# Up and down products with one 512-column matmul per weight tile, folded by ACT and DVE

## The reference, cut to what matters

```python
def _conv_ffn(h, w_up, conv_w, conv_b, w_down):
    a, g = jnp.split(h @ w_up, 2, axis=-1)
    a = lax.conv_general_dilated(a, conv_w[:, None, :], window_strides=(1,),
                                 padding=[(CONV_W - 1, 0)], dimension_numbers=('NWC', 'WIO', 'NWC'),
                                 feature_group_count=D_FF) + conv_b
    return (jax.nn.gelu(a) * g) @ w_down
...
y = _conv_ffn(h, w_up[l], conv_w[l], conv_b[l], w_down[l])
x = x + g2 * _rmsnorm(y, norm_g[l, 3])
```

## Time and profile before

| | us |
|---|---|
| median of three runs | 758.73 |
| lowest and highest | 753.63, 760.63 |
| span of the profiled execution | 757.1 |
| that execution's own time | not listed |
| PE busy (x5964) | 730.8 (97%) |
| PE weight loads busy | 710.5 (94%) |
| DVE busy | 524.7 (69%) |
| ACT busy | 396.1 (52%) |
| POOL busy | 104.3 (14%) |

### The profile page before, as it was taken

How to read it: one execution, slowest core, us unless ns; L and a number is a source line. 1 busy time by engine, 2 the same in 40 slices (tenths; PEclk the granted TensorE clock), 3 DMA queues, 4 the chain that set the end, 5 groups by cost and what they waited for, 6 DMA issues and landing times.

```text
span 757.1 us, 14222 instructions
## 1 busy us (share of the span) xinstructions
PE 730.8 (97%) x5964; PEld 710.5 (94%) x5964; DVE 524.7 (69%) x778; ACT 396.1 (52%) x560; POOL 104.3 (14%) x87
## 2 busy tenths in 40 slices
PE   8899999998899999999999999999999999999995
PEld 6799899898898999999999989899999999999995
DVE  4979888886977678777767556925576347555665
ACT  4286455545364544544544348528555456556551
POOL 0130000000522000000001130000004455443000
PEclk9999999999999999999999999979999999999998
DMA  8995567555363455654566544514446553343101
GB/s 343 411 356 190 203 268 274 193 204 219 113 244 146 167 200 190 213 178 161 204 261 233 205 138 148 207 66 168 167 154 223 184 206 117 116 159 112 57 1 56
DMA packets 22265, 141.13 MB, mean 186 GB/s; under 512 B 2389, under 2 KB 3029, under 8 KB 6458
## 3 DMA queue, kind: packets, MB, share of 16 engines
q1 hardware_dynamic: 21626, 137.28, 50.1%
q0 software_dynamic: 576, 2.95, 1.0%
HBM read 139.17 MB, written 1.05 MB: 185 GB/s over the span
## 4 chain that ended last, share of the span: by engine, by line
PE 70%; DVE 13%; issue 7%; ACT 5%; DMA 3%; POOL 0%; SPq 0%; DVEq 0%; ACTq 0%
PE res L1596 20%; PE res L1598 19%; PE res L1597 19%; ACT whi L639 3%; DVE wlo L1052 3%; PE pX L1803 2%; DMA shared<-in_w_ada 1%; PE pS L1783 1%; PE pX L1982 1%; DVE shared L1065 1%; DVE raw L1065 1%; DMA y<-in_w_ada 1%; ACT sq L654 1%; PE pT L1793 1%; PE pS L1644 1%
## 5 line engine op out<-in xcount | busy, mean ns | idle before, releaser
L1596 PE MATMUL res<-hhi,whi 128*128 128x256 f32 (+1 forms) x1120 | 318.9, 285 | 4.1 <-DVE wlo L1052 1.5
L1052 DVE TENSOR_TENSOR wlo<-raw,whi 128x2048 fp32r<-128x2048 f32 (+3 forms) x101 | 229.1, 2270 | 126.4 <-ACT whi L639 126.2
L1597 PE MATMUL res<-hhi,wlo 128*128 128x256 f32 (+1 forms) x1120 | 312.9, 279 | 0.0
L1598 PE MATMUL res<-hlo,whi 128*128 128x256 f32 (+1 forms) x1120 | 312.8, 279 | 0.0
L639 ACT ACTIVATE whi<-raw 128x2048 fp32r<-128x2048 f32 (+3 forms) x101 | 188.3, 1865 | 120.2 <-issue 87.1
L1596 PEld LDWEIGHTS res<-hhi,whi 128*128 128x128 f32 (+1 forms) x1120 | 209.6, 187 | 5.9 <-issue 3.4
L1597 PEld LDWEIGHTS res<-hhi,wlo 128*128 128x128 f32 (+1 forms) x1120 | 209.4, 187 | 0.4
L1598 PEld LDWEIGHTS res<-hlo,whi 128*128 128x128 f32 (+1 forms) x1120 | 209.4, 187 | 0.2
L538 POOL TENSOR_TENSOR sq<-sq,rope 128x512 f32<-128x512 f32 x18 | 39.5, 2195 | 78.5 <-ACT sq L654 78.5
L1596 PE MATMUL res<-uhi,whi 128*128 128x256 f32 x176 | 49.3, 280 | 0.0
L1597 PE MATMUL res<-uhi,wlo 128*128 128x256 f32 x176 | 49.1, 279 | 0.0
(11 more groups left out here) (334 smaller groups left out, 1211.1 us busy)
## 6 DMA issues: line engine op xcount, KB each, us to landing
raw<-in_wts SPq DMA_DIRECT2D x97, 1024.0 KB, 5.0
raw<-in_w_ada SPq DMA_DIRECT2D x16, 1024.0 KB, 5.1
shared<-in_w_ada SPq DMA_DIRECT2D x6, 1024.0 KB, 11.1
gates<-in_wts SPq DMA_DIRECT2D x4, 768.0 KB, 13.3
raw<-in_wts SPq DMA_DIRECT2D x4, 768.0 KB, 5.6
y<-in_w_ada SPq DMA_DIRECT2D x2, 1024.0 KB, 9.2
x<-in_xT SPq DMA_DIRECT2D x2, 512.0 KB, 4.7
gv<-in_ln_rows POOLq DMA_DIRECT2D x1, 1024.0 KB, 7.5
```

The source lines that it names most:

```text
L1052: nc.vector.tensor_tensor(lo[:, 0:b], raw[RAW_OF["w", c] % RAW][:, 0:b], hi[:, 0:b].bitcast(f32), ALU.subtract).then_inc(lo_ready, 1)
L1596: mm(out, ah, bh, start=first, stop=False)
L1597: mm(out, al, bh, start=False, stop=False)
L1598: return mm(out, ah, bl, start=False, stop=last)
```

## The change

- The up and down products use `wide` in place of `three`: one matmul of the high weights with the 512 columns [high input | low input] into a whole bank (A | B), and one of the low weights with the high input (256 columns) into A. For this the high and low tiles of each operand lie in one tensor (`hs`, `us`, `wsplit`, and others that are only renamed). The rest of the kernel keeps `three`.
- Bank places: even up chunks and even down blocks in pS (one bank per 128 outputs), odd ones in pT. PE waits for the drain two chunks (or two blocks) back.
- ACT copies the B halves to `side` (`copy_side`), DVE adds A and `side` (`fold`, `fold_up`): into `aseq`, into a new `gsum`, or into `y`. All results of up and down are now drained by DVE.
- ACT makes the first tap of the convolution (scale and bias), DVE the other two, those of the two tiles in turn, so that a tap doesn't wait for the one just ahead of it.
- In the steps of up DVE makes the low half of chunk b + 2 in place of b + 3, behind the fold, and `ulo` of a pair a step later than before.
- In down ACT squares and scales `y` in SBUF after the fold.
- `turned` at up chunk 2 is gone.

```diff
-    if c < MISC or BRANCH <= c < WOUT or (UP <= c < DOWN and (c - UP) % 2 == 1):
+    if c < MISC or BRANCH <= c < WOUT or UP <= c < GK:
         return "dve"
...
+        def wide_banks(c):
+            n = (c - UP) % 2 if c < DOWN else (c - DOWN) // 3 % 2
+            return (pS, pT)[n]
+        def wide_part(c, i, e):
+            return wide_banks(c)[:, :].rearrange("p (i e n) -> p i e n", i=2, e=2)[:, i, e, :]
...
+            def copy_side(c, i):
+                nc.scalar.activation(side_of(c)[:, i, :], wide_part(c, i, 1), ACT.Copy).then_inc(side_copied, 1)
+                if UP <= b < DOWN:
+                    act.wait_ge(product_done, RESULT_MARK[FIRST_RESULT[b]])
+                    if b >= UP + 2:
+                        act.wait_ge(drained_dve, RESULT_DRAIN[FIRST_RESULT[b - 2]][1])
+                    copy_side(b, slice(0, 2))
                 if b not in LATE and b not in (GOUT + 1, GOUT + 2) and b != WOUT + 2 and b >= DIRECT:
                     high(c + 2)
...
-                        nc.scalar.activation(aseq[:, j % 2, :, 2:T + 2], ps[:, :].rearrange("p (a b) -> p a b", a=2),
-                                             ACT.Copy).then_inc(drained_act, 1)
+                        act.wait_ge(drained_dve, RESULT_DRAIN[FIRST_RESULT[b]][1])
+                        for i in range(2):
+                            f = 2 * j + i
+                            nc.scalar.activation(conv[:, j % 2, i, :], aseq[:, j % 2, i, 0:T], ACT.Identity,
+                                                 scale=col("conv_w", f), bias=col("conv_b", f)).then_inc(conv_first, 1)
...
+                        act.wait_ge(product_done, RESULT_MARK[FIRST_RESULT[b] + i])
+                        if j >= 2:
+                            act.wait_ge(drained_dve, RESULT_DRAIN[FIRST_RESULT[b - 6] + i][1])
+                        copy_side(b, slice(i, i + 1))
+                    for i in range(2):
+                        act.wait_ge(drained_dve, RESULT_DRAIN[FIRST_RESULT[b] + i][1])
+                        nc.scalar.activation(sq[:, 2 * j + i, :], y[:, 2 * j + i, :], ACT.Square).then_inc(squares["n4"], 1)
...
+                        nc.scalar.activation(y[:, 2 * j + i, :], y[:, 2 * j + i, :], ACT.Copy,
+                                             scale=pcol[:, 3, 2 * j + i:2 * j + i + 1]).then_inc(y_scaled, 1)
...
+            def fold(c, i, dst):
+                return nc.vector.tensor_tensor(dst, wide_part(c, i, 0), side_of(c)[:, i, :], ALU.add)
+            def fold_up(c, dst):
+                dve.wait_ge(side_copied, copies(c))
+                fold(c, slice(0, 2), dst).then_inc(drained_dve, 1)
+                if UP <= b < DOWN:
+                    j = (b - UP) // 2
+                    if (b - UP) % 2 == 0:
+                        fold_up(b, aseq[:, j % 2, :, 2:T + 2])
+                        if j:
+                            u_low(j - 1)
+                    else:
+                        fold_up(b, gsum[:, :, :])
+                    if b > UP:
+                        low(c + 1)
+                if b == DOWN:
+                    u_low(FT // 2 - 1)
+                    low(c + 1)
...
-                            own(nc.vector.tensor_scalar(o, a[:, 0:T], col("conv_w", f), col("conv_b", f), ALU.mult, ALU.add))
-                            own(nc.vector.scalar_tensor_tensor(o, a[:, 1:T + 1], col("conv_w", FT + f), o, ALU.mult, ALU.add))
+                        for a, o, f in taps:
+                            nc.vector.scalar_tensor_tensor(o, a[:, 1:T + 1], col("conv_w", FT + f), o, ALU.mult, ALU.add
+                                                           ).then_inc(dve_self, 1)
+                        for i, (a, o, f) in enumerate(taps):
+                            dve_count[0] += 1
+                            dve.wait_ge(dve_self, dve_count[0])
+                            ins = nc.vector.scalar_tensor_tensor(o, a[:, 2:T + 2], col("conv_w", 2 * FT + f), o, ALU.mult, ALU.add)
...
-                        nc.vector.tensor_tensor(g, g, ps[:, :], ALU.mult).then_inc(drained_dve, 1)
+                        g = gelu[:, j % 2, :, :]
+                        nc.vector.tensor_tensor(g, g, gsum[:, :, :], ALU.mult).then_inc(u_full, 1)
...
+            def wide(out, a, b, first, last):
+                mm(out.rearrange("p (e n) -> p e n", e=2), a[:, 0, :], b, start=first, stop=False)
+                return mm(out[:, 0:T], a[:, 1, :], b[:, 0, :], start=False, stop=last)
+            def wide_half(c, i, k, inp, at):
+                return wide(wide_banks(c)[:, 512 * i:512 * i + 512], weights_of(c)[:, :, k, i * P:i * P + P], inp[:, :, k, :],
+                            at == 0, at == KT - 1)
...
                     elif c > UP + 1:
-                        if c == UP + 2:
-                            turned(c)
-                        fm(c, hhi, hlo)
+                        wait_weights(c)
+                        wait_drained(FIRST_RESULT[c - 2])
+                        for i in range(2):
+                            for k in range(KT):
+                                last = wide_half(c, i, k, hs, k)
+                        last.then_inc(product_done, 1)
                 elif c < GK:
...
+                    if kg == 0:
+                        wait_drained(FIRST_RESULT[UP + 20 + j] if j < 2 else FIRST_RESULT[DOWN] + 2 * (j - 2) + 1)
                     for i in range(2):
-                        ps = bank(r + i) if kg == 0 else res[(r + i) % NB]
+                        ps = wide_banks(c)[:, 512 * i:512 * i + 512]
...
-                            last = three(ps[:, 0:T], wh[:, k, i * P:i * P + P], wl[:, k, i * P:i * P + P],
-                                         uhi[:, kk, :], ulo[:, kk, :], kk == 0, kk == FT - 1)
+                            last = wide(ps, wp[:, :, k, i * P:i * P + P], us[:, :, kk, :], kk == 0, kk == FT - 1)
```

More of the change, by code:

```diff
@@ L296, in build @@
         with ExitStack() as st:
-            uhi = sb("uhi", [P, FT, T], f32r, at=st)
-            ulo = sb("ulo", [P, FT, T], f32r, at=st)
+            us = sb("us", [P, 2, FT, T], f32r, at=st)
+            uhi, ulo = us[:, 0, :, :], us[:, 1, :, :]
             aseq = sb("aseq", [P, 2, 2, T + 2], at=st)
@@ L1057, in result, with u_low @@
                 return place(r)
+            def fold(c, i, dst):
[3 more added lines that the diff above has]
+                fold(c, slice(0, 2), dst).then_inc(drained_dve, 1)
+            def u_low(j):
+                dve.wait_ge(u_hi, j + 1)
+                nc.vector.tensor_tensor(ulo[:, 2 * j:2 * j + 2, :], gelu[:, j % 2, :, :],
+                                        uhi[:, 2 * j:2 * j + 2, :].bitcast(f32), ALU.subtract).then_inc(u_lo, 1)
             def ada(a):
@@ L1241, in _ @@
                     unit_norm(2 * (c - ZG))
[L1242 removed]
+                if UP <= b < DOWN:
[11 more added lines that the diff above has]
+                    low(c + 1)
+                if DOWN <= b < GK and (b - DOWN) % 3 == 2:
+                    j = (b - DOWN) // 3
+                    for i in range(2):
+                        dve.wait_ge(side_copied, copies(b, i))
+                        fold(b, slice(i, i + 1), y[:, 2 * j + i:2 * j + i + 1, :]).then_inc(drained_dve, 1)
+                if (b not in LATE and not b < DIRECT and not UP <= b < DOWN and not GOUT <= b < SK and not b >= SOUT
+                        and not (b in RH and b > MISC)):
                     low(c + 2)
@@ new lines, in _ @@
+                        taps = [(aseq[:, j % 2, i, :], conv[:, j % 2, i, :], 2 * j + i) for i in range(2)]
+                        for a, o, f in taps:
[5 more added lines that the diff above has]
+                            ins = nc.vector.scalar_tensor_tensor(o, a[:, 2:T + 2], col("conv_w", 2 * FT + f), o, ALU.mult, ALU.add)
@@ L1592, in _, with three, wait_drained @@
             mm = nc.tensor.matmul
-            def three(out, ah, al, bh, bl, first, last):
-                mm(out, ah, bh, start=first, stop=False)
-                mm(out, al, bh, start=False, stop=False)
-                return mm(out, ah, bl, start=False, stop=last)
+            def three(out, a, b, first, last):
+                mm(out, a[:, 0, :], b[:, 0, :], start=first, stop=False)
+                mm(out, a[:, 1, :], b[:, 0, :], start=False, stop=False)
+                return mm(out, a[:, 0, :], b[:, 1, :], start=False, stop=last)
+            def wide(out, a, b, first, last):
[4 more added lines that the diff above has]
+                            at == 0, at == KT - 1)
+            def wait_drained(r):
+                who, n = RESULT_DRAIN[r]
+                pe.wait_ge(drained[who], n)
             def bank(r):
@@ L1615, in weights_of, with half_product, fm @@
                 kt, w = kt_of(c)
-                return tuple(h[:, 0:kt * w].rearrange("p (k n) -> p k n", k=kt) for h in halves(c))
-            def half_product(c, i, k, ps, ih, il, at, first=None, last=None):
-                wh, wl = weights_of(c)
```

(21 more changed lines are left out.)

156 lines of the change are left out of this document (74 added, 82 removed).

## The result

The changed kernel takes 761.62 us (median of 20 executions, 757.47 to 762.84), the kernel before 755.07 us (20 executions, 750.99 to 762.21): ratio 1.007, 95% interval 1.0046 to 1.0093. The forecast was 752.6 with a range to 760.5; the time lies beyond it. The three executions shown ahead (median 758.73) were not typical of the kernel before: of the 99 executions of it that were timed beside the other runs (the 12 of experiment 2 come on top, 9 and 3), 63 lie between 750.7 and 755.4 us (median 752.4) and 36 between 757.0 and 762.2 (median 759.1), with none in between. I call these the lower and the upper heap. The sum of the prediction was made against the upper one without knowing that there are two.

The account below looks back on a forecast made before the run. TensorE's back-to-back matmul starts were taken as the bound. Gains 8.8 + 0.35 less stalls 0.9, 1.1, 0.8 and 0.2 make 6.15 us, taken from 758.73: 752.6 us, range 749.5 to 760.5.

Parts of the forecast that it names:

- the row of plain f32 is the nearest: Up and down products: longer stream hides half the per-start excess; wide matmul 218.8 ns, 16.7 saved per triple, 8.8 us.
- The extra matmuls of `turned` go: 0.35 us.: Up chunk 2: three matmuls of 117.8 ns are dropped, a gain of 0.35 us.
- The base: Whole kernel: the 6.15 us gain was taken from 758.73 us, the median of three runs.
- Rival 3: Up and down products: excess goes by columns or moving-operand pieces, nothing saved; 760.5 us, chance 0.15.
- Rival 4: Up: the chain of copy, fold and low half becomes the bound, slower; 766.5 us, chance 0.10.
- Rival 1: Up and down products: 512 columns wholly hide a start's excess, 333.6 ns per triple; 751.1 us, chance 0.27.
- rival 2: Up and down products: every start keeps 11.1 ns, 342.2 ns per triple; 755.1 us, chance 0.18.
- Chunk 2: Entry of up: PE waits for copy and fold of chunk 0, as wide products have two bank places; 0.9 us.
- Chunk 3: Entry of up: PE waits for the low half, which stands behind DVE's taps and fold; 1.1 us.
- Down chunk 1: Entry of down: an adaLN row product on DVE delays the low half; stall 0.6 to 0.8 us.
- End of down: ACT's last square now stands behind copy, square, scale and fold, so k = 7 waits; 0.2 us.
- DVE's share in up: Up: added folds raise DVE's busy share from 77% to some 85%, ACT's to 65%.

Follow-up runs that it names:

- experiment 2: The kernel before, unchanged, profiled and timed again: 754.06 us (12 executions) beside 752.35 (17), ratio 1.0017.
- (1): A kernel without the layer, only streams of matmuls, each of one form: 120.0 ns for 256 columns, 226.7 for 512, pair 353.3.
- (4): The kernel before without `turned` at up chunk 2, run twice: 758.71 us (ratio 1.004) and 758.64 us (ratio 1.0035).
- experiment 5: Changed kernel with `turned` put back at up chunks 2 and 4: 762.14 us (1.0092) with three 256-column matmuls, 762.27 us (1.0102) with the wide one.
- (8): The changed kernel with two wide, then two narrow matmuls in place of one and one: 758.33 us, ratio 1.0037 to the kernel before.
- 6: The kernel before with `turned` at up chunks 2, 4, 6 and 8 instead of 2 alone: 755.12 us, ratio 0.9987.

## Why the prediction was wrong, point by point

- **The failed step: "the row of plain f32 is the nearest", 218.8 ns for the wide matmul.** Measured 234.0 ns, and 119.3 for the narrow one; saved 0 in place of 8.8 us. How much of the excess goes with a longer stream was taken from plain f32, and f32r doesn't do as plain f32 does: 512 f32r columns alone take 226.7 ns (1), an excess of 13.3 in place of the assumed 5.5, and 7 more when 256-column ones stand between (the first profile of the changed kernel). The stream has a period of its own, which depends on order and on how it started. The rows gave a warning: 117.8 and 113.4 ns for equal columns and equal loads were read as a sign that columns don't matter, and not as two rates of one kind of stream. In experiment 2 the 113.4 of the tokens-stationary matmuls is 117.7, so the difference said nothing of columns.
- **"The extra matmuls of `turned` go: 0.35 us."** Booked as a gain. They can change the rate of what follows; without them 6 of 24 executions were in the lower heap, with them 32 of 45 beside these (4). That is 0.46 x 6.7 us, some 3 us of the mean. The prediction took the price of their time alone, without asking what they did for what follows. With the wide pair, which has no faster rate in any profile here, it made no difference: put back they left the time at 762.3 (5).
- **The base.** The median of three, 758.73, was of the upper heap; of 99 executions the median is 753.6. A gain in the slower rate would have been measured against a kernel that is mostly in the faster.
- **Rival 3** gave 760.5 for nothing saved, and in the stage that is what happened, though not by its reasons: pieces cost nothing (1), and by its columns alone a pair would take 226.7 + 113.3 = 340.0 ns, not 353.3. That the median, 761.6, comes near its 760.5 is partly luck: its sum starts from 758.73, a time of the upper heap, and holds only because the changed kernel has no lower one. Rival 4 didn't come about: no steady stall. Rival 1's 215.8 ns and rival 2's 224 are the steady distance of no f32r stream.
- **The stalls,** from the last start ahead to the next, less the usual 0.12 us. Chunk 2: 0.96 us (forecast 0.9). Chunk 3: 0.76 (1.1); PE, saving nothing, came to it at 257.99 in place of 256.75, the low half at 258.70 in place of 257.85. Down chunk 1: none (0.8) at 353 ns a pair, and 0.16 as soon as a pair takes 345 (8). End of down: 0.6 (0.2). DVE's share in up is 75% (forecast some 85%), ACT's 62% (65%).
- **The sum as it came out.** Against the first profile of the kernel before, which had the slower rate too, the stage is 1.7 us longer: 0.96 and 0.76 at the two stalls, 0.3 for the slower first matmuls behind them and at the head of down, less 0.35 for `turned`. With 0.6 at the end of down it is 2.3 of the 2.7 us by which the span grew (757.1 to 759.8); another 0.3 lies ahead of the stage, which starts at 239.93 in place of 239.60. The rest of the difference of the medians is the lower heap, 6.7 us below, in which the changed kernel has no execution: there a triple takes 340.0 ns, and the wide pair's 353.3 is 13.3 more, 7.0 us over 528.

**Open.** What in a stream's start picks its rate: the profile shows distances, and in the kernel some starts lead to 113.3, more to 117.8, a few to 120.0 ns (around 730 us in the first profile of the kernel before, where the tokens are stationary). Streams alone were at 120.0 each time; why those of up and down are quicker wasn't found. That the wide pair never reaches 346.7 ns in the kernel is seen in the profiles of three kernels with it (the changed one, with `turned` put back, with the early low half); the changed kernel's executions from 757.5 to 760.3 us may have had it, but none of them was profiled. Why the share of the faster rate differs between chips is open as well.

## What to carry to other kernels

Price a new matmul shape in the order in which it will run, in a stream of its own: a shape's distance alone (226.7 ns) was 7 ns from its distance in the mix (234.0). Before costing against a profile, look whether the runs fall in heaps, and find out which heap the profile is of; compare shares only between executions timed side by side. A few matmuls that seem to do nothing may be there for what follows them; to cost their removal, look at the distances on both sides of them.

## What the runs showed of the hardware that was not expected

- An unbroken stream of f32r matmuls with 256 columns and 128 weight columns, at a granted clock of 1.00, has steady distances of 113.3 or 117.8 ns with the same instructions in up and down, and of 120.0 in streams alone. It kept one for as long as 180 us; behind a stall (experiment 5), and behind matmuls with the operands' roles exchanged (2, 6), it was another.
- Streams with 128 weight columns go no faster than 111.7 ns a matmul (128 and 192 columns); 512 columns take 226.7, which is 17/16 of their 512 cycles.
- 512 and 256 columns in turn: 353.3 or 346.7 ns a pair alone, 353.3 in every profile within the kernel; two and two: 345.0 within the kernel, 348.3 alone.
